# Output projection of an encoder layer as seven Strassen products of half length, with all weight low parts of the last three products on VectorE

## The reference

```python
mix = jnp.concatenate([na_out, ml_out], axis=-1)        # (1024, 2048)
x = x + jnp.einsum('bsm,md->bsd', mix, w_out[l])        # the output projection
h = rmsnorm(x, norm_ffn_g[l])
x = x + expert_choice_ffn(h, w_router[l], w_gate[l], w_up[l], w_down[l])
return rmsnorm(x, final_norm_g)
```

## Time and profile before

| | |
|---|---|
| median of 3 runs | 2692.42 us |
| profiled execution | 2693.19 us |
| its span (first to last instruction) | 2691.4 us |
| busy: TensorE, VectorE, ScalarE, GpSimd | 2649.8, 2067.9, 1463.2, 550.0 us |
| output projection | 1153.6 to 1541.0 us of the span |
| experts | 1570.4 to some 2660 us |

### The profile page before, as it was taken

How to read it: one execution, slowest core, us unless ns; L and a number is a source line. 1 busy time by engine, 2 the same in 40 slices (tenths; PEclk the granted TensorE clock), 3 DMA queues, 4 the chain that set the end, 5 groups by cost and what they waited for, 6 DMA issues and landing times.

```text
span 2691.4 us, 33672 instructions
## 1 busy us (share of the span) xinstructions
PE 2649.8 (98%) x12357; PEld 2187.4 (81%) x12357; DVE 2067.9 (77%) x2578; ACT 1463.2 (54%) x1717; POOL 550.0 (20%) x805
## 2 busy tenths in 40 slices
PE   9999999999999999999999989999999999999996
PEld 7888888888888888788888878888888888888885
DVE  7775776487777666864357499999999999999887
ACT  6433221122232267843232368888888888888776
POOL 1422111211111244811010121111111111111002
PEclk9999999999999999999999999999999999999998
DMA  9688876898888766434453499999999999999998
GB/s 363 245 284 301 274 265 211 283 347 279 282 302 285 263 215 215 157 132 164 142 175 134 151 418 394 392 406 406 404 405 402 406 403 405 404 404 403 398 404 375
DMA packets 251044, 827.49 MB, mean 307 GB/s; under 512 B 30326, under 2 KB 55429, under 8 KB 227853
## 3 DMA queue, kind: packets, MB, share of 16 engines
q1 hardware_dynamic: 210528, 685.12, 67.2%
q0 software_dynamic: 40352, 140.23, 15.0%
HBM read 727.90 MB, written 99.91 MB: 308 GB/s over the span
## 4 chain that ended last, share of the span: by engine, by line
PE 93%; DMA 1%; ACT 1%; DVE 1%; issue 1%; SPq 1%; POOL 0%; POOLq 0%; DVEq 0%; ACTq 0%
PE ps L3271 26%; PE ps L2900 6%; PE ps L2902 6%; PE ps L2901 6%; PE ps L2896 5%; PE ps L2897 5%; PE ps L2898 5%; PE ps L3116 4%; PE ps L3118 4%; PE ps L3117 4%; PE ps L3302 4%; PE ps L3301 4%; PE ps L3300 4%; PE ps L2951 1%; PE ps L3245 1%; PE ps L2839 1%
## 5 line engine op out<-in xcount | busy, mean ns | idle before, releaser
L2729 DVE TENSOR_TENSOR elo<-eraw,ehi 128x2048 fp32r<-128x2048 f32 x384 | 877.2, 2298 | 79.7 <-ACT ehi L1814 65.9
L1814 ACT ACTIVATE ehi<-eraw 128x2048 fp32r<-128x2048 f32 x384 | 733.3, 1920 | 215.4 <-PE ps L3271 133.3
L1442 ACT ACTIVATE whi<-raw 128x1024 fp32r<-128x1024 f32 x159 | 168.6, 1060 | 581.6 <-PE ps L2902 248.4
L3271 PE MATMUL ps<-ehi,xh 128*128 128x512 f32 x960 | 375.1, 391 | 0.0
L3271 PE MATMUL ps<-elo,xh 128*128 128x512 f32 x960 | 373.7, 389 | 0.0
L1932 DVE TENSOR_TENSOR wlo<-raw,whi 128x1024 fp32r<-128x1024 f32 x159 | 194.5, 1224 | 189.0 <-ACT whi L1442 188.6
L3271 PE MATMUL ps<-ehi,xl 128*128 128x512 f32 x960 | 256.6, 389 | 0.0
L3271 PEld LDWEIGHTS ps<-ehi,xl 128*128 128x128 f32 x960 | 180.2, 188 | 37.5
L3271 PEld LDWEIGHTS ps<-ehi,xh 128*128 128x128 f32 x960 | 180.2, 188 | 37.1
L3271 PEld LDWEIGHTS ps<-elo,xh 128*128 128x128 f32 x960 | 180.3, 188 | 36.9
L1700 ACT ACTIVATE ohi<-oraw 128x512 fp32r<-128x512 f32 x128 | 80.7, 631 | 237.9 <-PE ps L3118 237.8
(11 more groups left out here) (500 smaller groups left out, 5421.7 us busy)
## 6 DMA issues: line engine op xcount, KB each, us to landing
raw<-in_w_stream SPq DMA_DIRECT2D x271, 512.0 KB, 5.1
eraw<-in_w_gate SPq DMA_DIRECT2D x256, 512.0 KB, 8.0
eraw<-in_w_up SPq DMA_DIRECT2D x256, 512.0 KB, 10.1
eraw<-in_w_down SPq DMA_DIRECT2D x128, 1024.0 KB, 11.2
oraw<-in_w_stream SPq DMA_DIRECT2D x128, 256.0 KB, 2.6
xt<-in_xT SPq DMA_DIRECT2D x48, 256.0 KB, 4.2
scr_ops<-xt POOLq DMA_DIRECT2D x48, 256.0 KB, 3.3
nav<-scr_rows SPq DMA_DIRECT2D x128, 64.0 KB
```

The source lines that it names most:

```text
L1442: act.activation(whi[:, c % SPL, :], raw_pair(c)[0], ACT.Copy).then_inc(S["w_hi"], 1)
L1814: act.activation(ehi[:, p % ERING, :], flat2(eraw[:, 2 * (p % EDEEP):2 * (p % EDEEP) + 2, :]), ACT.Copy)\
L2729: dve.tensor_tensor(elo[:, p % ERING, :], flat2(eraw[:, 2 * (p % EDEEP):2 * (p % EDEEP) + 2, :]), ehi[:, p % ERING, :].bitcast(F32), ALU.s ...
L3271: last = pe.matmul(gu_bank(e, c), a[:, k, :], w[:, p % ERING, c * BW:(c + 1) * BW], start=(k == 0 and a is hi and w is ehi), stop=(k == KD ...
```

## The change

The mix is cut into four quarters (token halves by two sets `K1`, `K2` of eight slices) and the output weights into four (the same slices by even and odd column blocks). Seven products in the Winograd order of Strassen's scheme replace the eight of quarters. `OPROD` lists 14 steps: each product for two pairs of column blocks, eight slices each. Token sums are made in place of quarters that are done with; `op_upper` (ScalarE) writes their high parts and `op_lower` (GpSimd) their low parts. Weight sums are made on VectorE in the raw ring (`w_combine`: two operations per slice for p6, one for p7, p4 and p5, none for p1, p3 and p2); the sum of p6 is stored to memory and read again for p4. The low parts of weights are all made by VectorE: the list `LOW_P` of those that GpSimd would take is empty.

The products' results are added in several rows: `part_add`, `run_add`, `run_part` and `run_ahead` (VectorE) and `part_sum` (GpSimd) bring them together in `run0`, `run1` and in rows of `x`, which are stored to `x1` and loaded again (`store_part`, `fetch_x` by `OSTEPS` and `XAT`). The last addition for each of the eight blocks (`out_add`) is in steps 6 to 13; the router work of a block follows in the next step, packed into its eight slices (`TURNAT`, `OUTAT`, `LOWAT`, `LOGITAT`). The gain of the norm is no longer multiplied into the rows: it is multiplied into the router's matrix once and into the gate and up weights when they are split; `x1` and `h2` are stored from the same rows. The 47 top-k operations stand in steps 11 to 13 (`RANKAT`).

```diff
-KORD = [8, 9, 10, 11, 12, 13, 0, 1, 2, 3, 4, 5, 6, 7, 14, 15]
+K1, K2 = (8, 9, 10, 11, 12, 13, 0, 1), (2, 3, 4, 5, 6, 7, 14, 15)
+OTYPES = ("p1", "p6", "p7", "p4", "p5", "p3", "p2")
+OPROD = [(a, pair) for a in OTYPES for pair in range(2)]
+NS, KO = len(OPROD), KD // 2
+OPARTS = {"p1": ((0, 0),), "p6": ((1, 1), (0, 1), (0, 0)), "p7": ((1, 1), (0, 1)), "p4": ((1, 0), None),
+          "p5": ((0, 1), (0, 0)), "p3": ((1, 1),), "p2": ((1, 0),)}
+LOW_P = []
+TURNAT = [(2, 2, 3, 3) if f in (3, 6) else (2, 3, 4, 5) for f in range(OHB)]
+LOWAT = [(3, 3, 5, 5) if f in (3, 6) else (3, 4, 5, 6) for f in range(OHB)]
+LOGITAT = [(4, 4, 5, 5) if f in (3, 6) else (4, 5, 6, 6) for f in range(OHB)]
+RANKAT = {(11, k): 2 for k in range(3, 8)}
+RANKAT.update({(12, k): 3 if k else 1 for k in range(8)})
+RANKAT.update({(13, k): 3 if k else 1 for k in range(5)})
...
+                for part, at in enumerate(WPARTS[q]):
+                    if at:
+                        c, b = (K1, K2)[at[0]][k], 2 * pair + at[1]
+                        src = t["w_stream"][CPB * (BLK + b) + c // 2, :, (c % 2) * BW:(c % 2 + 1) * BW]
+                    else:
+                        src = t["w_sums"][pair, k, :, :]
+                    sp.dma_start(w_raw(q, part), src).then_inc(rawsem[q % ORING], 16)
...
+            def op_lower(ty, i):
+
+                pool.wait_ge(S["op_high"], BEFORE["op_high"] + KO * (ty - 1) + i + 1)
+                pool.tensor_tensor(mix_low(ty, i), mix_whole(ty, i), mix_high(ty, i).bitcast(F32), ALU.subtract).then_inc(S["op_low"], 1)
...
+            store_part(0)
+            for i in range(KO):
+                op_lower(1, i)
+            store_part(1)
+            part_sum(2)
+            store_part(2)
+            for i in range(KO):
+                op_lower(2, i)
+            part_sum(3)
+            store_part(3)
+            for i in range(KO):
+                second_sum(i)
+            for i in range(KO):
+                op_lower(3, i)
+            store_part(4)
...
+                if q in PARKED:
+                    act.dma_start(t["w_sums"][OPROD[q // KO][1], q % KO, :, :], oraw[:, q % ORING, :]).then_inc(parksem[q % ORING], 16)
...
+            def w_combine(q):
+
+                if not WSUM[q]:
+                    return
+                dve.wait_ge(rawsem[q % ORING], RAW0[q % ORING] + WLANDED[q])
+                a = w_raw(q, 0)
+                dve.tensor_tensor(a, a, w_raw(q, 1), ALU.subtract).then_inc(S["o_sum"], 1)
+                if WSUM[q] == 2:
+                    dve.wait_ge(S["o_sum"], BEFORE["o_sum"] + WSUMS[q] - 1)
+                    dve.tensor_tensor(a, a, w_raw(q, 2), ALU.add).then_inc(S["o_sum"], 1)
...
+            for q in range(ORING, NQO):
+                if q not in LOW_P:
+                    out_low(q)
+                if q + 1 < NQO:
+                    w_combine(q + 1)
+                (s, k), f = divmod(q - 3, KO), (q - 3) // KO - 1 - F0
...
+                if k == 0 and f >= 0:
+                    out_tiles(f)
+                elif k == 0 and s in (1, 2):
+                    part_add(s - 1)
+                elif k == 0 and s > 2:
+                    run_add(s - 1)
+                if k == 2 and s in (5, 6):
+                    run_part(s - 1)
+                if k == 4 and s in (5, 6):
+                    run_ahead(s - 5)
...
+                for c in range(4):
+                    if f >= 0 and LOWAT[f][c] == k:
+                        turned_low(f, c)
+                if f >= 0 and k == (6 if f == 3 else 7):
+                    out_logits(f)
...
+                for _ in range(RANKAT.get((s, k), 0)):
+                    if ranked < RANKS:
+                        rank(0, ranked)
+                        ranked += 1
...
+                pe.matmul(bank, mix_high(ty, k)[:, cut], hi, start=(k == 0), stop=False)
+                pe.matmul(bank, mix_high(ty, k)[:, cut], lo, start=False, stop=False)
+                return pe.matmul(bank, mix_low(ty, k)[:, cut], hi, start=False, stop=(k == KO - 1))
...
+                        if k == 0 and j == 0 and s >= 8:
+                            pe.wait_ge(S["o_lgout"], s - 7)
...
+                if kind == "gu":
+                    dve.scalar_tensor_tensor(out=elo[:, p % ERING, :], in0=raw_, scalar=mixg[:, k:k + 1],
+                                             in1=ehi[:, p % ERING, :].bitcast(F32), op0=ALU.mult, op1=ALU.subtract).then_inc(S["e_lo"], 1)
```

More of the change, by code:

```diff
@@ new lines, with x_loads, x_stored @@
+PART_V, PART_P = (0, 1, 4, 5, 9, 11), (2, 3)
+FINAL_N = [n for n, x in enumerate(OSTEPS) if x[3] is not None]
+def x_loads(n):
+    return sum(x[4] == OSTEPS[n][4] for x in OSTEPS[:n + 1])
+def x_stored(n):
+    return sum(64 if x[3] is None else 128 for x in OSTEPS[:n + 1] if x[4] == OSTEPS[n][4])
+TURNS = [("na", 0, 1), ("na", 1, 1), ("na", 0, 0), ("na", 1, 0)] + [("na", k, 0) for k in range(2, 8)] + [("ml", 0, 0), ("ml", 1, 0)]
+TURNS += [("na", k, 1) for k in range(2, 8)] + [("ml", 2, 1), ("ml", 3, 1)]
@@ new lines, in fetch_x @@
+            def fetch_x(n):
+                s, g, b, f, slot, src = OSTEPS[n]
+                before = [m for m in range(n) if OSTEPS[m][4] == slot]
+                if n < 2:
+                    sp.wait_ge(S["asm_tr"], 12 + 16 + 4)
+                if before:
+                    sp.wait_ge(ox1stsem[slot], x1st0[slot] + x_stored(before[-1]))
+                    done = OSTEPS[before[-1]][3]
+                    if done is not None:
+                        sp.wait_ge(S["o_tr"], 4 * done + 4)
+                        sp.wait_ge(S["o_sq"], BEFORE["o_sq"] + 4 * done + 4)
+                if src is not None:
+                    sp.wait_ge(ox1stsem[OSTEPS[src][4]], x1st0[OSTEPS[src][4]] + x_stored(src))
+                rows = t["x" if src is None else "x1"].rearrange("(n p) c -> p n c", p=P)
+                sp.dma_start(oxs[:, slot, :, :], rows[:, 4 * g:4 * g + 4, b * BW:(b + 1) * BW]).then_inc(oxinsem[slot], 16)
@@ new lines, in _ @@
+            store_part(0)
[13 more added lines that the diff above has]
+            store_part(4)
+            for i in range(KO):
+                op_summed(4, i)
@@ new lines, in _ @@
+            store_part(5)
+            store_final(0)
+            for i in range(KO):
+                op_lower(4, i)
+            store_final(1)
+            for i in range(KO):
+                op_summed(5, i)
+            store_final(2)
+            store_part(9)
+            for i in range(KO):
+                op_lower(5, i)
+            store_final(3)
+            store_part(11)
+            row_scales_of(0)
+            for i in range(KO):
+                op_lower(6, i)
+            place_constants()
@@ L1329, in _ @@
+            store_final(4)
+            for q in LOW_P[:3]:
+                out_lower(q)
+            store_final(5)
+            for q in LOW_P[3:7]:
+                out_lower(q)
+            store_final(6)
+            for q in LOW_P[7:]:
+                out_lower(q)
+            store_final(7)
+            row_scales_of(1)
             place_columns()
@@ L2602, in tile_low @@
+            turned_low(OHB - 2, 2)
+            turned_low(OHB - 2, 3)
+            while ranked < RANKS:
+                rank(0, ranked)
+                ranked += 1
+            dve.tensor_copy(best[:, 1, :], besti[:, 0, :]).then_inc(S["affn"], 1)
             def tile_low(j):
@@ L3150, in _ @@
[L3150 to L3152 removed]
+                    if s == 0:
+                        for n in range(3 * k, min(3 * k + 3, len(TURNS))):
+                            turn_mix(n)
+                    for c in range(4):
+                        if f >= 0 and TURNAT[f][c] == k:
+                            turn(f, c)
+                        if f >= 0 and LOGITAT[f][c] == k:
+                            logits(f, c)
```

565 lines of the change are left out of this document (332 added, 233 removed), and 3 rows, old and new, of the table OSTEPS.

## The result

The changed kernel takes **2712.2 us** (median of 4 runs, 2710.0 to 2713.9) against 2692.1 for the kernel before on the same chip (4 runs): a ratio of 1.0074, 95% interval 1.0057 to 1.0091. It is slower by 20 us, where 21 us less were forecast. The profiled execution took 2713.9 us, span 2712.2.

What follows compares the result with a forecast made beforehand. TensorE, busy 98% of the span, was taken as the bound. The terms -43.7 - 0.7 + 10 + 4 + 4 + 1 + 4 = -21.4 us, off the median of 2692.42, gave 2671 us, range 2651 to 2692.

Steps and rivals of the forecast that it cites:

- The 192 matmuls: Output projection: 1344 matmuls instead of 1536, at 0.2278 us each, take 43.7 us off the path.
- The ranks: Steps 11 to 13: 47 top-k operations moved there load VectorE and stall TensorE by 4 us (1 to 7).
- GpSimd's price per operation beside VectorE: Projection: a VectorE operation with two SBUF inputs is blocked 1.1 of the 1.28 us of a GpSimd operation.
- VectorE's load, blocked time included: Steps 1 to 7: 108 + 1 + 56 x 1.1, corrected to 167 us with 3 us idle, against 157 of matmuls.
- I take 10 us (0 to 24): Steps 1 to 7: stall from VectorE's load, GpSimd's blocking included, exceeding the time of the matmuls.
- 4 us for steps 8 to 10: Steps 8 to 10: GpSimd's operations fall on the last slices, one blocked operation too many each time; 0 to 9.
- The lead: Projection: parts are made three slices ahead, so VectorE falling up to about 7 us behind costs nothing.
- my sign for "forecast wrong": The forecast is wrong if TensorE's waits in the stage sum to under 8 or over 40 us, or an expert lengthens.
- DMA: Around p6: 19.7 MB of weight pieces, parked sums and partial rows exceed the queues' rate; 4 us (0 to 8).
- the row load: Step 6: partial-row load at slice 53 waits on SyncE for a late store, delaying weights; 1 us (0 to 4).
- C: Rival: shared read path decides, GpSimd operations of 1.7 us or more beside VectorE, stalls of 59, 2707 us; chance 0.08.
- B: Rival: first half port-bound, VectorE hardly idle, GpSimd's operations cost it their full 1.28 us; stalls 42, 2690 us; chance 0.15.

Runs made afterwards that it cites:

- experiment 5: Changed kernel with GpSimd's 80 new operations only writing and the weight sums of p6 not parked in memory: 2658.0 us.
- experiment 7: Changed kernel with nine of the weight low parts of steps 11 to 13 made by GpSimd instead of VectorE: 2707.2 us.
- experiment 1: Changed kernel with GpSimd's 80 new two-input operations replaced by fills with zero of the same tiles: 2670.5 us.
- Experiment 8: Changed kernel with each of GpSimd's 72 operand operations waiting for one more weight low part, meant as at most one per slice: 2694.7 us.
- Experiment 6: Changed kernel with only the 24 operand sums moved from GpSimd to VectorE, one per slice: 2703.3 us.
- experiment 4: Changed kernel with VectorE's 80 weight sums working on 16 of 512 columns, their waits kept: 2693.7 us.
- experiment 10: Changed kernel with all 80 operand and partial operations on VectorE and nine weight low parts of steps 11 to 13 on GpSimd: 2671.1 us.

## Why the prediction was wrong

**What held.** The 192 matmuls: the stage of experiment 5 is 350.6 us, and 387.4 - 43.7 = 343.7, plus 5.3 in step 6 and 2.6 for the ranks, gives 351.6. (The 0.7 us of the gain multiply belong behind the stage. The stretch from its end to the first expert took 29.3 us where it took 29.4, so no run shows that term.) The ranks: forecast 4 (1 to 7), measured 2.6 by experiment 7. The experts: 68.2 us each. GpSimd's price per operation beside VectorE: forecast 1.1 us, measured 1.77 - 0.69 = 1.08 where they take turns. Even VectorE's load, blocked time included, held: for steps 1 to 7 the working gave 164 us of work, and the windows above sum to 166.4.

**The step that failed** is the one after that: "I take 10 us (0 to 24)" for steps 1 to 7 and 4 us for steps 8 to 10. The 10 came from VectorE's load of 167 us with its idle start against the 157 us of the matmuls, as if work could be poured into any gap. The seven steps took 202.0 us with VectorE busy for 166.4, so it was idle for 36 of them and TensorE waited all the same. Of the 45 us lost there, 28.2 go with GpSimd's operations (experiment 1), above the upper end of 24; the rest is mostly the terms for the DMAs. Steps 8 and 9 lost another 12.6, and experiment 1 gives these back in full, where 4 was the price. In all it puts GpSimd's operations at 40.7 us, against my 14. Two things were left out of the sum:

- *Runs.* A blocked operation of VectorE was priced at one operation of GpSimd. When GpSimd has its inputs ready it goes through a run, and VectorE can stand still for all of it: 10.9 us for eight. The lead that I said "costs nothing" (7 us) is then gone at a stroke, and sum, high part and low part of the next slices follow one after the other on two engines, so VectorE's idle time behind it can't be used. Experiment 8, with the same work spaced, gives 15.4 of the 40.7 us back. Experiment 6 moves all three runs of sums to VectorE: that repairs step 8 (7.7 us), but the stage gains only 10.5. The remaining 25 us I put down to taking turns, 1.1 us each in steps where VectorE was wanted, and to the bunches left in experiment 8; this is argued, and no run divides these.
- *What a wait costs beyond its length.* TensorE was idle for 40.4 us of the stage (403.7 less 363.3 busy) against 5.2 in experiment 5; the other 17.9 us of the difference is the same matmuls taking longer (363.3 against 345.4). The lower clock is at most 14.6 of it: the granted clock was 0.89 to 0.94 in steps 2, 3 and 6 to 9. But steps 4 and 5 had a granted clock of 1.00 and hold 3.3 us of the 17.9 (busy 23.68 and 23.14, where a clean step has 21.76). I had priced each wait at its own length, and the sum has no term for this. So my sign for "forecast wrong" (waits over 40 us) was just met, and the time lost was nearly half as much again.

**DMA, forecast 4 (0 to 8), and the row load, 1 (0 to 4).** Parking alone was worth 12.4 us without GpSimd's reads and 7.7 with them; the row load in step 6 5.3 us. Both mechanisms were in the text and both were too small by 4 to 8 us. The bytes were about right (steps 2 and 3 moved 19.2 MB by their GB/s, forecast 19.7, at shares of 0.96 and 0.87), but I treated the parked sum as bytes only and not as a landing for which the ring slot waits (41.1 us of SyncE's waits). These terms alone would have left the change faster: 350.6 + 12.4 is the 363.0 us stage of experiment 1, at 2670.5 us.

**The rivals.** C came near the time (2707) and named the shared path, deciding from about 1.4 us per operation of GpSimd; the 80 had a mean of 1.48 us. But its mechanism, VectorE with 204 us of work, did not come: VectorE had 166, so that the number is near is luck. I had dismissed it by an operation's own length, which was the wrong test; a chain of operations can be late without any engine being full. B also has VectorE hardly idle, and it was idle for 36 us of the seven steps. Its ends summed to 52 us, and were cut to 42 because waits would hide each other; measured were 60 (403.7 less 343.7).

The Trainium skill, page SBUF — State Buffer, section "Who interferes with whom", says that a GpSimd instruction which only writes does not contend with a VectorE instruction of two SBUF inputs. Experiment 1 agrees (VectorE's low parts at 691 ns beside 80 memsets). The same page of the Trainium skill, section "SBUF: two separate sides", says that whichever of the two starts first gets the shared pair for its whole instruction. I read that as a bound of one instruction, 1.28 us here, by which I priced. The trace differs from it: VectorE's operation started 0.4 us before the run of eight, and it ended after all of them, at 10.9 us.

**Left open.** Why GpSimd's run in step 8 shut VectorE out while the one in step 6 let it take turns; the traces show both, in experiment 4 the shutting out in step 6 as well, and not the reason. Whether parking costs by its bytes or by its landing. What sets step 3 where all sums are on VectorE: its 38 operations (24 us of 21.8) fit the 31 us only in part. Parking is the rival: without GpSimd's reads step 3 fell from 29.6 us (experiment 1, VectorE busy for 18.2) to 21.8 when nothing was parked (experiment 5). All sums on VectorE with nothing parked was not run. An operation of GpSimd that reads but is as short as the memset was not tried.

## What to carry to other kernels

Before giving a two-input operation to GpSimd, count what it takes from VectorE: here 0.6 us saved against 1.1 us blocked, so keeping it on VectorE won 35 us. The exception was nine low parts, one every second slice, beside the top-k work in the last steps (2.5 us won), where no low part of VectorE took over 0.73 us (experiment 10). If GpSimd must have it, tie each operation to the pace of the consumer, so that no run forms. And do not compare sums of busy time with the bottleneck's time where several engines hand one slice on to each other: add the longest single hold, compare it with the lead, and price each wait of TensorE beyond its own length.

## What the runs showed of the hardware

- One VectorE operation with two SBUF inputs (0.69 us) lasted 10.90 us beside eight back-to-back GpSimd operations (9.95 us); another lasted 5.74 us beside four. One over 16 columns (median 0.17 us) lasted 10.72 us (experiment 4). The same kind in turns: 1.77 us on VectorE and 1.65 on GpSimd. Adds with one input in PSUM never left 0.67 to 0.69 us.
- Behind a 6.0 us wait TensorE ran at a granted clock of 0.51 for 4.3 us; over the stage, 40 us of waits came with 18 us of slower matmuls, 3.3 of them in steps with a granted clock of 1.00.
- The DMA queues carried 353 GB/s at a share of 0.99 in step 2 of experiment 5 without making TensorE wait.
